# Output and down projections with tokens on partitions, layer norm by token tiles

## The reference, cut to what matters

```python
for i in range(DEPTH):
    m = forgetting_attention(x, ...) if i % 2 == 0 else rglru_block(x, ...)   # ends in o @ w_out
    x = layer_norm(ALPHA * x + m, ln1_g[i], ln1_b[i])
    ff = conv_ffn(x, ...)            # up 1024 -> 2 x 2816, causal conv of 3, gelu(gate) * val, @ w_down
    x = layer_norm(ALPHA * x + ff, ln2_g[i], ln2_b[i])
    gate = sigmoid(x @ ple_gate_w[i] + ple_gate_b[i])
    x = x + gate * (p[i] @ ple_w[i])
```

## Time and profile before

| what | value |
|---|---|
| median of 3 runs (all: 1373.12, 1373.19, 1378.39) | 1373.19 us |
| profiled execution: time, span | 1378.74 us, 1377.0 us |
| PE busy | 1319.0 us, 96% |
| PE weight loads busy | 1033.3 us, 75% |
| DVE, ACT, POOL busy | 601.7, 437.4, 914.1 us |
| granted TensorE clock, mean | 0.979 |
| DMA | 116.33 MB, mean 84 GB/s |

### The profile page before, as it was taken

How to read it: one execution, slowest core, us unless ns; L and a number is a source line. 1 busy time by engine, 2 the same in 40 slices (tenths; PEclk the granted TensorE clock), 3 DMA queues, 4 the chain that set the end, 5 groups by cost and what they waited for, 6 DMA issues and landing times.

```text
span 1377.0 us, 18552 instructions
## 1 busy us (share of the span) xinstructions
PE 1319.0 (96%) x5780; PEld 1033.3 (75%) x5780; DVE 601.7 (44%) x878; ACT 437.4 (32%) x703; POOL 914.1 (66%) x1289
## 2 busy tenths in 40 slices
PE   6999999988999999999999699998999999999998
PEld 3666666666888888888878577776888888888876
DVE  6533444275444444413253357175544444313263
ACT  1434343313334333300043257114433433201042
POOL 6434443374798777687876555483987887678854
PEclk9999999996999999999999899998999999999999
DMA  4111111111233232233223222211332332333321
GB/s 177 49 61 46 61 61 46 61 62 61 77 107 107 91 98 84 82 101 98 87 106 122 67 78 70 77 62 61 107 107 91 98 100 74 99 97 86 119 77 61
DMA packets 34024, 116.33 MB, mean 84 GB/s; under 512 B 3728, under 2 KB 5008, under 8 KB 33984
## 3 DMA queue, kind: packets, MB, share of 16 engines
q1 hardware_dynamic: 33008, 113.26, 25.6%
q10 hardware_dynamic: 976, 2.55, 0.5%
HBM read 113.63 MB, written 2.16 MB: 84 GB/s over the span
## 4 chain that ended last, share of the span: by engine, by line
PE 60%; issue 19%; POOL 10%; POOLq 7%; DVE 3%; DVEq 1%; DMA 1%; ACT 0%; SPq 0%; ACTq 0%
PE bank L370 17%; PE bank L372 17%; PE bank L371 17%; POOL w_lo L356 9%; POOLq L353 4%; POOLq L351 2%; PE bank L587 2%; PE bank L590 2%; PE bank L588 2%; PE bank L394 1%; DMA stage<-w_square 1%; DVEq L802 1%; DVE part_total L801 1%; DVE x L790 0%; DVE dist L759 0%
## 5 line engine op out<-in xcount | busy, mean ns | idle before, releaser
L356 POOL TENSOR_TENSOR w_lo<-stage,w_hi 128x256 fp32r<-128x256 f32 (+1 forms) x848 | 643.3, 789 | 31.2 <-issue 0.9
L370 PE MATMUL bank<-x_hi,w_hi 128*128 128x512 f32 x896 | 357.9, 399 | 3.2 <-POOL w_lo L356 1.6
L371 PE MATMUL bank<-x_lo,w_hi 128*128 128x512 f32 x896 | 349.2, 390 | 0.0
L372 PE MATMUL bank<-x_hi,w_lo 128*128 128x512 f32 x896 | 349.1, 390 | 0.0
L350 POOL TENSOR_TENSOR waiter<-waiter 128x1 f32<-128x1 f32 x212 | 46.6, 220 | 382.0 <-PE bank L372 264.3
L352 POOL TENSOR_SCALAR w_hi<-stage 128x1024 fp32r<-128x1024 f32 (+1 forms) x212 | 223.0, 1052 | 33.7 <-issue 33.7
L370 PEld LDWEIGHTS bank<-x_hi,w_hi 128*128 128x128 f32 x896 | 168.5, 188 | 48.0 <-issue 15.9
L372 PEld LDWEIGHTS bank<-x_hi,w_lo 128*128 128x128 f32 x896 | 168.3, 188 | 36.0
L371 PEld LDWEIGHTS bank<-x_lo,w_hi 128*128 128x128 f32 x896 | 168.6, 188 | 31.8
L949 DVE SCALAR_TENSOR_TENSOR tmp<-bank,cols,tmp 128x511 f32<-128x511 f32 x88 | 66.0, 750 | 197.3 <-ACT tmp L1208 186.3
L370 PE MATMUL bank<-h_hi,w_hi 128*128 128x512 f32 x352 | 139.7, 397 | 0.0
(11 more groups left out here) (188 smaller groups left out, 1795.4 us busy)
## 6 DMA issues: line engine op xcount, KB each, us to landing
stage<-w_square SPq DMA_DIRECT2D x164, 512.0 KB, 3.3
stage<-w_down SPq DMA_DIRECT2D x32, 448.0 KB, 3.3
stage<-w_down SPq DMA_DIRECT2D x16, 512.0 KB, 3.5
outT<-x SPq DMA_DIRECT2D x8, 256.0 KB, 2.0
x<-xT SPq DMA_DIRECT2D x2, 512.0 KB, 5.1
x<-xT ACTq DMA_DIRECT2D x2, 512.0 KB, 8.4
p_in<-pT ACTq DMA_DIRECT2D x2, 512.0 KB, 3.4
w_ai<-w_lru SPq DMA_DIRECT2D x1, 1024.0 KB, 6.1
```

What stands on the lines that cost most here:

```text
L356: low = pool.tensor_tensor(w_lo[:, s, to], stage[:, s, to], w_hi[:, s, to].bitcast(F32), ALU.subtract)
L370: pe.matmul(out, w_hi[:, s, c:c + P], m_hi, start=first, stop=False)
L371: pe.matmul(out, w_hi[:, s, c:c + P], m_lo, start=False, stop=False)
L372: return pe.matmul(out, w_lo[:, s, c:c + P], m_hi, start=False, stop=last)
```

## The change

It turns the output and down projections around: 128 tokens (four tiles t) lie on the partitions, the activations are loaded and 512 output channels of weights stream as four runs of 128. Each projection has two halves of 512 channels; a bank holds one token tile of one half, eight banks in all. A weight unit of these two phases is now two k blocks of four output tiles, read in 1 KB pieces. In the second half of out, and for the last six of 22 k blocks of down's second half, the token tiles are done one after another. The output projection's second four units are split into `far_hi` and `far_lo`, apart from the ring of four.

The layer norm then runs along the free axis: DVE adds the residual in the bank, takes statistics (`bn_stats`, `bn_aggr`), ACT the root, DVE centres with the gain row and scales with the bias row (`rows`, loaded by SP for each norm). PE turns each tile back with four transposes (`turn_tile`), ACT copies the bank to `x_hi` and DVE makes `x_lo`. After the second norm of a layer ACT also copies the turned `x` back (`channel_rows`); before a first norm `x` itself has to be turned to tokens: eight blocks in the first projection of qkv and eight around the first gate (`turn_block`, `token_block`). The mean and sum matmuls of PE, the shift and the squares go. The gate's loop is written out on ACT and PE, and PE starts rgx with six tiles through. down, ple, gate, rgx, rgg and out are no longer loops on SP and POOL, and these phases drop POOL's `waiter` instruction. `next_hi` and `next_lo` become `in_hi` and `in_lo`, `mix_hi` and `mix_lo` share the place of `x_hi` and `x_lo`.

```diff
+    ring, apart = [3, 0, 1, 2], [7, 4, 5, 6]
+    want = [("qkv", [0, 1, 2], PAIRS)]
+    for layer in range(DEPTH):
+        if layer:
+            want += [("rgx", ring * 2, 1), ("rgg", ring * 2, 1)]
+        want += [(f"out{layer}", ring + apart, 1), (f"up{layer}", ring, 2 * FT // 4),
+                 (f"down{layer}", ring * (FT // 4) + ring[:FT % 4], 1), (f"ple{layer}", ring[FT % 4:], 1),
+                 (f"gate{layer}", ring * 2, 1)]
...
+            def norm_rows(n):
+                if n == 0:
+                    sp.wait_ge(flat_stored, 16)
+                else:
+                    sp.wait_ge(norm_ready, n * 2 * QT)
+                src = rows_dram[n // 2, (n % 2) * 16:(n % 2) * 16 + 16, :].rearrange("a n -> (a n)")
+                sp.dma_start(rows[:].rearrange("p a n -> p (a n)"),
+                             src.partition_broadcast(P)).then_inc(rows_loaded, 16)
...
+                        to = stage[:, s, :]
+                        if name.startswith("down") or name.startswith("out"):
+                            half, kp = r // (n // 2), r % (n // 2)
+                            w, u = (w_down, layer * KT + half * 4) if name.startswith("down") else \
+                                (w_square, base + half * 4)
+                            src = w[u:u + 4, :, kp * 2 * P:(kp + 1) * 2 * P].rearrange("a p n -> p a n")
+                            to = to.rearrange("p (a n) -> p a n", a=4)
...
+                        high, low = (w_hi, w_lo) if place_at < SLOTS else (far_hi, far_lo)
...
+            def token_three(out, w_at, c, m_hi, m_lo, first, last):
+                high, low = (w_hi, w_lo) if w_at < SLOTS else (far_hi, far_lo)
+                wide_hi = high[:, w_at % SLOTS, :].rearrange("p (a b n) -> p a b n", a=4, b=2)[:, :, c, :]
+                wide_lo = low[:, w_at % SLOTS, :].rearrange("p (a b n) -> p a b n", a=4, b=2)[:, :, c, :]
+                pe.matmul(four(out), m_hi, wide_hi, start=first, stop=False)
+                pe.matmul(four(out), m_hi, wide_lo, start=False, stop=False)
+                return pe.matmul(four(out), m_lo, wide_hi, start=False, stop=last)
+            def turn_tile(n, t, half):
+                pe.wait_ge(norm_ready, low_of(n, t, half))
+                for a in range(4):
+                    mm = pe.transpose(ln_bank(n, t, half)[:, a * P:(a + 1) * P],
+                                      x[:, 4 * half + a, t * P:(t + 1) * P], ident[:])
+                mm.then_inc(turn_done, 1)
...
-            def norm_sums(n):
...
-            def norm_spread(n):
...
+            def second_half_out(layer, n):
+                beside = {(2, 0): (0, 0), (2, 1): (0, 1), (3, 1): (1, 0), (3, 2): (1, 1)}
+                for t in range(QT):
+                    for k in range(KT):
+                        if (t, k) in beside:
+                            turn_tile(n, *beside[t, k])
+                        if t == 0 and k % 2 == 0:
+                            unit_ready(phases[f"out{layer}"], 0, 4 + k // 2)
+                        mm = out_step(layer, 1, t, k)
+                        if t == QT - 1 and k % 2 == 1:
+                            mm.then_inc(unit_used, 1)
+                    if t < QT - 1:
+                        mm.then_inc(sum_done, 1)
+                turn_tile(n, 2, 0)
+                turn_tile(n, 2, 1)
+                turn_tile(n, 3, 0)
...
+            def square_phase(name, n, at_banks, last_turn, bank_free):
...
+                pe.wait_ge(ln_hi, low_of(n, QT - 1, 0))
+                for k in range(4):
+                    for r in range(3):
+                        high_step(k, r)
+                    if k == 1 and last_turn is not None:
+                        last_turn()
+                pe.wait_ge(ln_lo, low_of(n, QT - 1, 0))
+                for k in range(4):
+                    for r in range(3):
+                        low_step(k, r)
+                pe.wait_ge(ln_hi, low_of(n, QT - 1, 1))
+                pe.wait_ge(ln_lo, low_of(n, QT - 1, 1))
+                for r in range(3):
+                    for k in range(4, KT):
+                        high_step(k, r)
+                        low_step(k, r)
+                for k in range(KT):
+                    high_step(k, 3)
+                    low_step(k, 3)
...
+            def down_phase(layer, n):
+                ph = phases[f"down{layer}"]
...
+                beside = {(2, 2): (0, 0), (2, 4): (0, 1)}
+                for t in range(QT):
+                    for k in range(together, FT):
+                        if (t, k - together) in beside:
+                            turn_tile(n, *beside[t, k - together])
+                        if t == 0 and k % 2 == 0:
+                            unit_ready(ph, 0, FT // 2 + k // 2)
...
+            def embed_and_turn(layer, n):
+                ple_tile(layer, 0)
+                turn_tile(n, 1, 0)
+                turn_tile(n, 1, 1)
+                for m in (1, 2, 3):
+                    ple_tile(layer, m)
+                turn_tile(n, 2, 0)
+                turn_tile(n, 2, 1)
+                for m in (4, 5, 6):
+                    ple_tile(layer, m)
+                turn_tile(n, 3, 0)
+                ple_tile(layer, 7)
+                turn_tile(n, 3, 1)
+            def gate_phase(layer, n):
+                name = f"gate{layer}"
+                square_phase(name, n, [banks[b] for b in GATE_BANK], None,
+                             lambda r: pe.wait_ge(tile_read[f"ple{layer}"], 5 + r))
+                for r in range(4, 8):
+                    pe.wait_ge(tile_read[name], r - 3)
+                    beside = {}
+                    if layer == 0 and r >= 6:
+                        beside = {k: (lambda m=m: next_block(m)) for k, m in zip((1, 3), (2 * r - 12, 2 * r - 11))}
+                    whole_tile(phases[name], 0, r, GATE_BANK[r % 4], x_hi, x_lo, beside)
+            def next_block(m):
+                pe.wait_ge(tile_read["gate0"], m + 1)
+                if m == 0:
+                    pe.wait_ge(x_back, low_of(0, QT - 1, 1))
+                if m >= 4:
+                    pe.wait_ge(x_tok_ready, KT + m - 3)
+                turn_block(m, NEXT_BANK[m % 4])
...
-            pe.wait_ge(tile_read["gate0"], 4 + KT)
-            pe.wait_ge(x_lo_ready, 3 * KT + 1)
-            rg_tile("rgx", 0, 0, {k: (lambda k=k: pe.wait_ge(x_lo_ready, 3 * KT + k + 2)) for k in range(KT - 1)})
-            rg_tile("rgx", 1, 1)
+            pe.wait_ge(tile_read["gate0"], KT - 2)
+            pe.wait_ge(x_lo_ready, KT + 1)
+            rg_tile("rgx", 0, 0, {k: (lambda k=k: pe.wait_ge(x_lo_ready, KT + k + 2)) for k in range(KT - 1)})
+            pe.wait_ge(tile_read["gate0"], KT)
...
+            def summed(n, layer, half, t):
+                ph = phases[f"out{layer}" if n % 2 == 0 else f"down{layer}"]
+                if t < QT - 1:
+                    dve.wait_ge(sum_done, (n * 2 + half) * (QT - 1) + t + 1)
+                else:
+                    dve.wait_ge(unit_used, ph.done(0, (half + 1) * len(ph.slots) // 2 - 1))
+                bank = ln_bank(n, t, half)
+                dve.scalar_tensor_tensor(four(bank), block_of(x, t, half), ALPHA, four(bank), ALU.mult, ALU.add)
+                dve.drain()
+                dve.bn_stats(norm_stat[:, t, half * 6:half * 6 + 6], bank[:])
+                dve.drain()
+            def centred(n, t, half):
+                bank = ln_bank(n, t, half)
+                gain = rows[:, 0, half * SEQ:(half + 1) * SEQ]
+                dve.scalar_tensor_tensor(bank[:], bank[:], norm_stat[:, t, 12:13], gain, ALU.subtract, ALU.mult)
+                dve.drain()
+            def normed(n, t, half):
+                bias = rows[:, 1, half * SEQ:(half + 1) * SEQ].rearrange("p (a n) -> p a n", a=4)
+                dve.scalar_tensor_tensor(block_of(x, t, half), four(ln_bank(n, t, half)), norm_stat[:, t, 15:16],
+                                         bias, ALU.mult, ALU.add).then_inc(norm_ready, 1)
+            def norm_low(n, t, half):
+                dve.wait_ge(ln_hi, low_of(n, t, half))
+                dve.tensor_tensor(block_of(x_lo, t, half), four(ln_bank(n, t, half)),
+            def layer_norm(n, layer):
+                if n % 2 == 0:
+                    dve.wait_ge(x_tok_ready, (layer + 1) * KT)
                 for t in range(QT):
+                    summed(n, layer, 0, t)
+                dve.wait_ge(rows_loaded, 16 * (n + 1))
+                for t in range(QT):
+                    summed(n, layer, 1, t)
+                    dve.bn_aggr(norm_stat[:, t, 12:14], norm_stat[:, t, 0:12]).then_inc(var_ready, 1)
+                    if t in (1, 2):
+                        norm_low(n, t - 1, 0)
+                        norm_low(n, t - 1, 1)
                     dve.drain()
+                    centred(n, t, 0)
+                    dve.wait_ge(dev_ready, n * QT + t + 1)
+                    dve.reciprocal(norm_stat[:, t, 15:16], norm_stat[:, t, 14:15])
                     dve.drain()
```

(71 more changed lines are left out.)

572 lines of the change are left out of this document (233 added, 339 removed).

## The result

The median is 1329.64 us (four runs, 1329.32 to 1330.12); the kernel before, with one run more than in the table above, has 1375.79 (1373.12 to 1382.08). The ratio is 0.966, 95% interval 0.962 to 0.970. The forecast was 1333. The profiled execution took 1330.12 us against 1378.74 before: 48.6 us less, where the sum said 39.9.

The account below looks back on a forecast made before the run. TensorE was taken as the bound, with gains only where it waits, runs at the lower clock or does other work. 13.3 + 8.5 + 7.0 + 10.2 + 4.8 - 3.9 = 39.9 us gave 1333 us median, range 1315 to 1358.

Parts of the forecast that it names:

- the sum: Whole kernel: gains of all parts less the cost at the start, 39.9 us saved.
- the output norm of layer 0: Norm behind layer 0's output projection: only the last token tile's norm stays exposed, gain 13.3 us.
- the down norms: Norms behind the down projections: 8.0 us of PE work removed, transposes and a short wait added; gain 3.5 each, 7.0.
- the start: Kernel start: eight turned blocks and a PE wait for ACT cost 3.9 us, between 2 and 7.
- the gate: Gate to RG-LRU input: PE's wait and lower clock go, less eight turned blocks; gain 10.2 us, between 5 and 11.
- the gapped stream: Rival, 0.06: output and down matmuls streaming four runs of 128 act as four short ones; 173 us more, 1506.
- the 1 KB pieces: Rival, 0.03: weight transfers in 1 KB pieces cost four times a 4 KB row's share; 132 us, 1465.
- the transposes' length: Rival, 0.04: each transpose costs PE its full length, not its spacing; 32 us more, 1365.
- no PE wait for split weights in layer 1: Expected sign in layer 1: PE never waits there for weights split by POOL.
- the 4.8 for the weights: Layer 1, before the output projection: PE no longer asks for four split units at once; gain 4.8 us.
- the 8.0: Each norm behind a down projection: PE time removed with the shift, sum and spreading matmuls, 8.0 us.
- DVE as the bound: Rival, 0.09: DVE's 512-wide norm steps slow beside POOL's splitting and bound the norms; 42 us, 1375, half of it 1354.

Follow-up runs that it names:

- contig: Changed kernel with output and down weights laid out by the host so 512 streamed channels lie in one run, in 4 KB rows: 1329.48 us.
- turn_twice: Changed kernel with the four transposes of each of the norms' 32 turned tiles done twice: 1338.28 us.
- not_apart: Changed kernel with the second four output weight units put back into the four slots that the first four use: 1336.14 us.
- stats_twice: Changed kernel with the norm statistics taken twice on each of the 32 half tiles: 1334.83 us.

## Why the prediction was right, point by point

**The sum.** 39.9 was said and 48.6 measured in the profile; the medians differ by 46.1. Every term has the right sign. The 8.7 us too little lie in three terms: the output norm of layer 0 (4.1) and the down norms (3.9), both with losses of before that were not listed, and the start (1.6); the gate takes back 1.3. The median of 1333 came out nearer (3.4 us off) than the sum did, and that is luck: 5.5 us were taken off because the profiled run of before was a long one, while that of after lies only 0.5 above its median.

**Spacing and transposes.** 0.229 for the down matmuls in both kernels; four transposes hold PE 0.36 us. The rivals of the gapped stream, of the 1 KB pieces and of the transposes' length are refuted by contig and turn_twice. The gapped stream was rightly put at nothing.

**Output norms.** The chain came out nearly as worked out: statistics 0.70 (0.69 taken), DVE's steps from residual to scaling 3.65 us (310.64 to 314.29; 3.8 said, with 0.2 of latency), DVE late by 0.4 us where 1 was said, a stop of 5.7 us against 5 to 7 said. The cost was 11.9 us against 10.6, the difference being the wait for POOL that I had not seen: I counted how long splitting takes, not when POOL is let go. So the sign "no PE wait for split weights in layer 1" failed: there is one of 0.86 us, in its up projection. For layer 1 the term and the 4.8 for the weights together said 13.3, and 13.6 came. In layer 0 13.3 was said and 17.4 came, though the cost was 1.3 higher: 5.4 us to be explained. The step that failed is the loss of before: I counted from the point where the dense stream breaks, 309.25, and PE had waited within the second half already:

```profile
277.11 0.47 PE L587 MATMUL bank<-mix_hi,w_hi 128*128 128x512 f32 x1 [0.86 <-issue]
...
286.10 1.12 PE L388 MATMUL bank<-part_total,shift_of 128*128 128x512 f32 x2 [1.19 <-DVEq L808]
...
287.43 0.47 PE L370 MATMUL bank<-mix_hi,w_hi 128*128 128x512 f32 x1 [0.21 <-POOL w_lo L356]
...
293.93 0.47 PE L370 MATMUL bank<-mix_hi,w_hi 128*128 128x512 f32 x1 [0.75 <-POOL w_lo L356]
...
300.22 0.47 PE L370 MATMUL bank<-mix_hi,w_hi 128*128 128x512 f32 x1 [0.54 <-POOL w_lo L356]
```

By the full timeline, PE's own matmuls start 1.0, 2.7, 0.9 and 0.7 us later at these four places than they were due; 0.8 of that is the shift matmul, which the sum had. The other 4.5 us are most of the 5.4. Three of the rows are waits for split weights, of the kind that not_apart brings back. The 4.8 us for layer 1 were not measured apart from the norm. Their reason, that PE no longer asks for four units at once, is borne out by not_apart: without the place of their own no wait comes back in layer 1, since the 3.08 us of before lay at the start of the first half, which units 4 to 7 do not touch.

**Down norms.** 3.5 each was said, 5.45 came. Two waits of PE at the embedding tiles of before, with their restarts 0.47 and 0.57 us, were not in the 8.0; PE now waits 0.23 us there, not 1. The term's mechanism stands: the matmuls of the old norm are gone and the eight turned tiles of a norm cost about what was said for them (turn_twice: 0.38 us for the four transposes more, 0.43 said with the restart).

**Gate to RG-LRU.** No wait and no lower clock is left, as said; 8.9 came for 10.2; the wider spacing of the RG-LRU matmuls on `in_hi` (384 x 4 ns = 1.5 us) accounts for the difference. Half of the reason was wrong: the staggered start, to which I gave 5.5 us of the chain's time, is worth 0.7 us once PE asks for six tiles only.

**Start.** The first scores come 3.5 us later (45.00 against 41.49; 3.9 said). By the first output matmul only 2.3 are left, though QKV's spacing has widened by about 2 us in all (576 matmuls, 0.230 to 0.2333): a 1.6 us wait in the attention of before is gone, and the rest of that gain was not traced.

**DVE as the bound.** Refuted as priced: its 512-wide steps take 0.69 to 0.75 beside POOL. But stats_twice shows how near it was: 0.2 us to spare a tile.

**Not run.** The change also unrolls loops on SP and POOL and drops POOL's `waiter` in these phases. No run undoes that alone, so its share in the stages' gains is not known.

## What to carry to other kernels

A norm over an operand that is finished tile by tile costs little more than its last tile's chain, as long as a tile's norm takes no longer than the next tile's matmuls (6.2 against 6.4 us here). So order the producing loop such that tiles finish one after another: 24 us of stops went here by order alone. List the losses before by comparing the stage's whole length with matmuls times spacing, not from the longest gaps: what was missed lay in short waits. And when work is given its own buffers, look for the waits that are written for the old ones: a loop's single lead held POOL back for 20 us.

## What the runs showed of the hardware

The spacing of equal fp32r matmuls depends on where the operands lie in SBUF: 0.2267 us at best; 448 bytes past a multiple of 512 from the first buffer, 0.2289 if it is the loaded operand (`h_hi` in down) and 0.233 if it is the streamed one (`in_hi`, `far_hi`, `p_hi`); 320 bytes past, 0.229 for the streamed one (before's `h_hi`, `p_hi`, `next_hi`). Moving the buffers by 64 bytes, to a multiple of 512, gives back 4.9 us. The change itself had lost part of that: QKV's input went from a multiple of 4096 to such a place and RG-LRU's from 320 to 448 past, about 2 and 1.5 us over their 576 and 384 matmuls.

Statistics of 128 x 512 f32 read from PSUM take 0.70 us, as long as an elementwise row of that size (the residual, 0.69).

Four 128 x 128 f32 transposes against the identity, between dense matmuls, hold PE 0.36 us and eight 0.79 us, though each is 0.28 us long.
